# A trunk of two layers: weights split on ScalarE and VectorE in output projection and feed-forward, and norm products behind the up tiles

## The reference, cut to what matters

```python
for i in range(2):
    h = rms_norm(x, norm_g[i, 0])
    y = mixer(h)                          # ends with "@ w_out", 1024 x 1024
    x = x + rms_norm(y, norm_g[i, 1])     # "post" of sites 1 and 3
    y = conv_ffn(rms_norm(x, norm_g[i, 2]), ...)     # "pre" of sites 1 and 3
    x = x + rms_norm(y, norm_g[i, 3])     # "post" of sites 2 and 4

def conv_ffn(h, w_up, conv_w, conv_b, w_down):        # w_up 1024 x 5632, w_down 2816 x 1024
    u = causal_depthwise_conv(h @ w_up, conv_w, width=3) + conv_b
    val, gate = split(u, 2)
    return (gelu(gate) * val) @ w_down
```

## Time and profile before

| | us |
|---|---|
| median of 3 runs | 3966.37 |
| lowest and highest | 3961.04, 3982.27 |
| the profiled execution | 3962.33 |
| its span, first to last instruction | 3960.5 |
| TensorE busy | 3225.2 (81% of the span) |
| VectorE busy | 2469.7 (62%) |
| GpSimd busy | 1405.3 (35%) |
| ScalarE busy | 1367.3 (35%) |
| mean granted TensorE clock | 0.894 of full |

### The profile page before, as it was taken

How to read it: one execution, slowest core, us unless ns; L and a number is a source line. 1 busy time by engine, 2 the same in 40 slices (tenths; PEclk the granted TensorE clock), 3 DMA queues, 4 the chain that set the end, 5 groups by cost and what they waited for, 6 DMA issues and landing times. The chain is left out here.

```text
span 3960.5 us, 49368 instructions
## 1 busy us (share of the span) xinstructions
PE 3225.2 (81%) x16664; PEld 2657.6 (67%) x16664; DVE 2469.7 (62%) x3835; ACT 1367.3 (35%) x2987; POOL 1405.3 (35%) x1041
## 2 busy tenths in 40 slices
PE   7889989999879899879956401888888789998897
PEld 5778878888767777767744301766667668786786
DVE  5455555556278686678765698444442787867556
ACT  4255544445222222222234442444441322222222
POOL 2300000000356666657520000001015566775663
PEclk8699998899989999999987755989899899998998
DMA  4100000002322223223220000000023222232232
GB/s 150 43 1 16 16 18 16 16 16 96 107 68 87 75 85 96 81 73 91 80 77 11 11 0 0 16 32 16 32 96 122 69 80 85 85 96 75 84 101 77
DMA packets 281285, 237.45 MB, mean 60 GB/s; under 512 B 8533, under 2 KB 258071, under 8 KB 280599
## 3 DMA queue, kind: packets, MB, share of 16 engines
q1 hardware_dynamic: 279959, 233.17, 19.0%
q10 hardware_dynamic: 1152, 2.10, 0.1%
HBM read 205.88 MB, written 27.26 MB: 59 GB/s over the span
## 5 line engine op out<-in xcount | busy, mean ns | idle before, releaser
L377 PE MATMUL PS<-HH,WH 128*128 128x512 f32 x2160 | 896.1, 415 | 78.0 <-DVE HL L519 23.0
L366 POOL TENSOR_TENSOR WL<-WR,WH 128x1024 fp32r<-128x1024 f32 x335 | 873.1, 2606 | 27.9
L378 PE MATMUL PS<-HL,WH 128*128 128x512 f32 x2160 | 865.4, 401 | 0.0
L379 PE MATMUL PS<-HH,WL 128*128 128x512 f32 x2160 | 862.3, 399 | 0.0
L377 PEld LDWEIGHTS PS<-HH,WH 128*128 128x128 f32 x2160 | 422.3, 196 | 170.5 <-issue 57.2
L362 POOL TENSOR_TENSOR TOUCH<-WR 128x1 f32<-128x1 f32 x335 | 126.6, 378 | 1091.8 <-PE PS L379 893.2
L379 PEld LDWEIGHTS PS<-HH,WL 128*128 128x128 f32 x2160 | 420.3, 195 | 91.6
L378 PEld LDWEIGHTS PS<-HL,WH 128*128 128x128 f32 x2160 | 422.5, 196 | 85.2 <-issue 5.1
L363 POOL TENSOR_SCALAR WH<-WR 128x1024 fp32r<-128x1024 f32 x335 | 383.1, 1144 | 0.7 <-issue 0.3
L645 PE MATMUL PS<-m_KDH,m_QS 128*128 128x512 f32 (+2 forms) x192 | 93.0, 484 | 247.0 <-ACT m_PX L835 197.3
L978 POOL TENSOR_TENSOR n_ROT<-n_ROT,n_SIN 128x512 f32<-128x512 f32 x15 | 19.1, 1273 | 699.5 <-ACT n_ROT L617 699.5
(11 more groups left out here) (344 smaller groups left out, 6984.6 us busy)
## 6 DMA issues: line engine op xcount, KB each, us to landing
WR<-in_ffn_w_up SPq DMA_DIRECT2D x176, 512.0 KB, 3.8
WR<-in_ffn_w_down SPq DMA_DIRECT2D x88, 512.0 KB, 3.5
WR<-in_nsa_w_out SPq DMA_DIRECT2D x16, 512.0 KB, 3.8
WR<-in_dsa_w_in SPq DMA_DIRECT2D x16, 512.0 KB, 4.7
WR<-in_dsa_w_out SPq DMA_DIRECT2D x16, 512.0 KB, 3.9
WR<-in_nsa_w_in SPq DMA_DIRECT2D x15, 512.0 KB, 5.5
HH<-oh_save SPq DMA_DIRECT2D x2, 3584.0 KB, 12.5
HL<-ol_save SPq DMA_DIRECT2D x2, 3584.0 KB, 21.6
```

The source lines that it names most:

```text
L366: nc.gpsimd.tensor_tensor(WL[:, s, :], WR[:, r, :], WH[:, s, :].bitcast(F32), ALU.subtract).then_inc(w_split, 1)
L377: nc.tensor.matmul(dst, wh, xh, start=start, stop=False)
L378: nc.tensor.matmul(dst, wh, xl, start=False, stop=False)
L379: return nc.tensor.matmul(dst, wl, xh, start=False, stop=stop)
```

## The change

Output projection and feed-forward: GpSimd splits only the first three tiles of each output projection. For every other tile ScalarE copies the high part (`high_split_act`) and VectorE subtracts (`low_split_dve`), both written into their orders three tiles ahead: behind the eviction and the convolution of up tile t, and, for the second and third up tile of the next step, behind the down evictions. The tiny operation of line 362 falls away there. In attention and layer entry GpSimd goes on, its first tile waiting for the one before it.

Norm products of the feed-forward, and the output transposes, stand behind the up tiles of a step instead of ahead of them. The product of the second half's post norm moves from behind the first up tile to step 0, with its root and reciprocal. In the output projection the norm product of the pre norm stands behind k = 13 instead of 12, and VectorE's and ScalarE's norm work is cut up and chained to the tiles.

```diff
+        def high_split_act(act, info):
+            r, x = info["raw"], info["split"]
+            act.wait_ge(w_raw[r], info["landed"])
+            act.wait_ge(*info["free"])
+            act.wait_ge(w_hi, info["n"])
+            nc.scalar.activation(WH[:, x, :], WR[:, r, :], ACT.Copy).then_inc(w_hi, 1)
+
+        def low_split_dve(dve, info):
+            r, x = info["raw"], info["split"]
+            dve.wait_ge(w_hi, info["n"] + 1)
+            dve.wait_ge(w_split, info["n"])
+            nc.vector.tensor_tensor(WL[:, x, :], WR[:, r, :], WH[:, x, :].bitcast(F32),
+                                    ALU.subtract).then_inc(w_split, 1)
...
-                if k == DT + 4:
+                if k == DT + 5:
                     stat_pe(pe, 2 * n + 1, "pre", 0)
...
+            squares, highs = {2: (0, 3), 3: (3, 6), 4: (6, 8)}, {6: (0, 4), 7: (4, 8)}
...
                 nc.scalar.activation(Y[n][:, m, tokens(hf)], bank(k % 4), ACT.Copy).then_inc(out_ev, 1)
+                high_split_act(act, after_outproj(a, n, k))
...
+            applies, sums = {1: (0, 4), 2: (4, 8)}, {3: (1, 3), 4: (3, 8)}
+            products = {6: (0, 4), 7: (4, 8)}
+            for k in range(2 * DT):
+                hf, m = k // DT, k % DT
+                low_split_dve(dve, after_outproj(a, n, k))
+                if m:
+                    sum_dve(dve, site, "post", hf, m)
...
+                if m in applies:
+                    post_apply_dve(dve, site, 0, *applies[m])
+                for dt in range(*sums.get(m, (0, 0))):
+                    sum_dve(dve, site, "pre", 0, dt)
+                if m == 5:
+                    reciprocal_dve(dve, site, "pre", 0)
+                if m in products:
+                    d0, d1 = products[m]
+                    for dt in range(d0, d1 + 1):
+                        if dt < d1:
+                            pre_apply_dve(dve, site, 0, dt)
+                        if dt > d0:
+                            low_dve(dve, site, 0, dt - 1)
...
-                if g == 0 and t == 0:
-                    stat_pe(pe, 2 * n + 1, "post", 1)
...
         def ffn_pe(pe, n):
             up_pe(pe, n, 0)
             for g in range(GROUPS):
-                if g in STAT_POST and g:
+                if g + 1 < GROUPS:
+                    up_pe(pe, n, g + 1)
+                if g in STAT_POST:
                     stat_pe(pe, step_site(n, g), "post", STAT_POST[g])
...
-                if g + 1 < GROUPS:
-                    up_pe(pe, n, g + 1)
                 down_pe(pe, n, g)
...
+                    if ffn_place(g) + t + 3 < TILES:
+                        high_split_act(act, ffn_tile(n, ffn_place(g) + t + 3))
...
+            if ffn_place(g) + t + 3 < TILES:
+                low_split_dve(dve, ffn_tile(n, ffn_place(g) + t + 3))
...
                     up_act(act, n, g + 1)
+                    for b in range(ffn_place(g + 1) + 7, min(ffn_place(g + 1) + 9, TILES)):
+                        high_split_act(act, ffn_tile(n, b))
...
                     down_dve(dve, n, g, 5, 8)
+                    for b in range(ffn_place(g + 1) + 7, min(ffn_place(g + 1) + 9, TILES)):
+                        low_split_dve(dve, ffn_tile(n, b))
                     hidden_low_dve(dve, n, g + 1, 1)
...
-                    if g:
-                        reciprocal_dve(dve, site, "post", 0)
+                    reciprocal_dve(dve, site, "post", STAT_POST[g])
                     post_apply_dve(dve, site, STAT_POST[g], 0, 4)
```

More of the change, by code:

```diff
@@ L352, in load, with split @@
             sp.dma_start(dst, src).then_inc(w_raw[info["raw"]], 16)
-        def split(pool, info, it=0):
+        def split(pool, info, it=0, after=False):
             r, s = info["raw"], info["split"]
+            if after:
+                pool.wait_ge(w_split, info["n"])
             pool.wait_ge(w_raw[r], at(info["landed"], it))
@@ L1062, in outproj_pe, with after_outproj, outproj_act @@
                     stat_pe(pe, 2 * n + 1, "post", 0)
-                if k == DT + 4:
+                if k == DT + 5:
                     stat_pe(pe, 2 * n + 1, "pre", 0)
-        def outproj_act(act, n):
+        def after_outproj(a, n, k):
+            return a.infos["out"][k + 3] if k + 3 < 2 * DT else ffn_tile(n, k + 3 - 2 * DT)
+        def outproj_act(act, a, n):
             site = 2 * n + 1
+            squares, highs = {2: (0, 3), 3: (3, 6), 4: (6, 8)}, {6: (0, 4), 7: (4, 8)}
             for k in range(2 * DT):
@@ L1076, in outproj_act @@
                     root_act(act, site, "post", 0)
[L1077 to L1080, removed]
+                for dt in range(*squares.get(m, (0, 0))):
+                    pre_square_act(act, site, 0, dt)
+                if m == 5:
                     root_act(act, site, "pre", 0)
-                if m in (5, 6):
-                    for dt in range(4 * (m - 5), 4 * (m - 4)):
-                        high_act(act, site, 0, dt)
@@ L1086, in outproj_dve @@
-        def outproj_dve(dve, n):
+                for dt in range(*highs.get(m, (0, 0))):
+                    high_act(act, site, 0, dt)
+        def outproj_dve(dve, a, n):
             site = 2 * n + 1
-            for dt in range(1, DT):
-                sum_dve(dve, site, "post", 0, dt)
-            reciprocal_dve(dve, site, "post", 0)
[L1091 to L1107, removed]
+            applies, sums = {1: (0, 4), 2: (4, 8)}, {3: (1, 3), 4: (3, 8)}
[5 more added lines that the diff above has]
+                    sum_dve(dve, site, "post", hf, m)
+                if hf == 0:
+                    continue
+                if m == 0:
+                    reciprocal_dve(dve, site, "post", 0)
+                if m in applies:
+                    post_apply_dve(dve, site, 0, *applies[m])
+                for dt in range(*sums.get(m, (0, 0))):
+                    sum_dve(dve, site, "pre", 0, dt)
+                if m == 5:
+                    reciprocal_dve(dve, site, "pre", 0)
[6 more added lines that the diff above has]
+                            low_dve(dve, site, 0, dt - 1)
@@ L1137, in trunk, with ffn_tile, ffn_place @@
         APPLIES = {4: (1, 0, 3), 5: (1, 3, 6), 6: (1, 6, 8), 16: (0, 0, 3), 17: (0, 3, 6), 18: (0, 6, 8)}
+        def ffn_tile(n, b):
+            kind, g, c = ffn_order()[b]
+            return F[n][kind][g][c]
+        def ffn_place(g):
+            return 0 if g == 0 else 4 + 6 * (g - 1)
+        TILES = len(ffn_order())
         def step_site(n, step):
@@ L1386, in ffn_sp @@
                     load(sp, p["down"][g][c], wd[tile + c])
-        def ffn_pool(pool, n):
-            for kind, g, c in ffn_order():
-                split(pool, F[n][kind][g][c])
         def columns(w, col):
@@ L1730, in prep1_pool @@
         def prep1_pool(pool):
-            for x in L1["c"] + [L1["i0"]]:
+            split(pool, L1["c"][0], after=True)
+            for x in L1["c"][1:] + [L1["i0"]]:
                 split(pool, x)
@@ L2196, in _ @@
             attention_pool(pool, A0)
-            for x in L0["out"]:
+            for x in L0["out"][0:3]:
                 split(pool, x)
-            ffn_pool(pool, 0)
             prep1["pool"](pool)
             attention_pool(pool, A1)
-            for x in L1["out"]:
+            for x in L1["out"][0:3]:
                 split(pool, x)
-            ffn_pool(pool, 1)
         @block.scalar
@@ L2220, in _ @@
             attention_act(act, A0)
-            outproj_act(act, 0)
+            outproj_act(act, A0, 0)
             ffn_act(act, 0)
@@ L2224, in _ @@
             attention_act(act, A1)
-            outproj_act(act, 1)
+            outproj_act(act, A1, 1)
             ffn_act(act, 1)
```

7 lines of the change are left out of this document (2 added, 5 removed).

## The result

| | before | after |
|---|---|---|
| median | 3966.37 us (three runs; with the one taken beside the change 3963.7, 3948.67 to 3982.27) | 3804.78 us (four runs, 3791.11 to 3808.72) |
| ratio | | 0.9567, 95% interval 0.9528 to 0.9606 |
| profiled execution | 3962.33 | 3804.23 |
| its span | 3960.5 | 3802.4 |
| first up tile to last down, layers 0 and 1 | 825.9, 813.8 | 739.3, 741.6 |

The kernel became 4.3% faster. The forecast was 3820 us; the median lies inside the range of 3795 to 3875, the ratio applied to the 3966.4 of before gives 3794.6, just under its low end. The mechanism was right, the gain was under-sized: 143 us forecast, some 172 by the ratio (interval 156 to 187). The medians are nearer to each other, 3804.78 for 3963.7 (159 us), which lies at the low end of that interval.

What follows compares the result with a forecast made beforehand. TensorE was taken as the bound in a good step, with stalls and late downs as removable excess. Gains of 74 and 59 us in the feed-forwards and 10 in the projections made 143: 3820 us predicted, range 3795 to 3875.

Steps and rivals of the forecast that it cites:

- the sum of the new excess: Feed-forward time above 22 stall-free steps: 26 us left of 100.3 in layer 0, 29 of 88.2 in layer 1.
- The exclusion between GpSimd and VectorE: VectorE operations with two SBUF operands end only after GpSimd's 2.70 us subtraction, so its busy time is partly waiting.
- All stalls at norm products go: Feed-forward: all six TensorE stalls, 15 us each, covered by 21.8 us of up products; each product still costs 0.75.
- The charge for evictions: Third down eviction of a feed-forward step, slack 0.1 us: charged 0.3 us a step, 6 us a layer.
- Late downs in steps 1 and 13: Feed-forward: down starts 2 us late and loses 2.5 to the clock, 4.5 in each step, 9 a layer.
- The end of the feed-forward: Wait and low clock at the last down product, 7 us a layer before; 6 us a layer charged as remaining.
- Output projection: Stall moves rather than goes: 6.8 us at k = 13, normalized half complete at 61.6; gain 5 a layer, bounds -4 and 9.
- Third eviction late: Rival, 12%: the queue between second and third down eviction loses 1.4 us in each of 42 steps: 3866 us.
- Saturated by busy time: Rival, 3%: VectorE's 28 us a step are real work, 35 with the change, so it is the bound: 3852 us.
- Norm product waits elsewhere: Rival, 4%: sums still late behind the up tiles, so six stalls of 15 less the split's gain remain: 3905 us.
- Slower: Rival, 4%: VectorE becomes the bound if a subtraction of 1024 takes 2.7 us: 4018 us; decides from about 2.5 us.
- Better: Case, 10%: steps 1 and 13 lose nothing and the projection gains 9: 3794 us.

Runs made afterwards that it cites:

- the run with work nobody needs: Changed kernel plus two unused GpSimd subtractions of 640 columns per feed-forward weight tile: 4008.75 us, ratio 1.0102 to before.
- the one with the subtraction on GpSimd: Changed kernel with GpSimd instead of VectorE subtracting for the weights' low part, ScalarE still copying: 3893.73 us, ratio 0.9816 to before.
- the order alone: Kernel before, with only the feed-forward's up tiles moved ahead of norm products and transposes, GpSimd still splitting: 3914.57 us, ratio 0.9885.
- The longer subtraction: Changed kernel with half of each VectorE weight subtraction (512 columns) made once more ahead of it: 3878.19 us, ratio 0.976 to before.
- the split alone: Changed kernel with the feed-forward's norm products and output transposes ahead of the up tiles again: 3898.91 us, ratio 0.982 to before.
- the products one tile earlier: Changed kernel with all eight pre-norm products of the output projection directly behind the reciprocal, before tiles 14 and 15: 3773.41 us, ratio 0.9524 to before.
- the subtraction made twice: Changed kernel with each whole VectorE weight subtraction (1024 columns) made twice: 4024.73 us, ratio 1.0131 to before.

## Why the mechanism was right, and which terms were mis-sized

The step that failed is in the sum of the new excess, 26 us in layer 0 and 29 in layer 1, which came out at 13.7 and 16.0. Three of its terms were too large. The evictions were charged with 6 us a layer and cost 0.4; the late downs of steps 1 and 13 were charged with 9, 2.5 each of it for the clock, and cost 3.2 with no clock in it; the end was charged with 6 and waited 3.06 and some 2.5. What was to go, and why, was as forecast.

*The exclusion between GpSimd and VectorE: shown.* It was read from one pair of rows; the run with work nobody needs (204 us) shows it by itself, and the one with the subtraction on GpSimd (89 us) agrees, though a part of its price is that GpSimd's subtraction is longer. The Trainium skill (GPSIMD Engine Reference, Specifications) names the two parties; what the exclusion costs only the rows tell.

*The split hides: right.* Subtraction 1.21 assumed, 1.222 measured; copy 1.11 assumed, 1.063 measured. The down tiles' subtractions come in time in every good step, as walked.

*All stalls at norm products go: right,* and each product costs 0.86 us for the 0.75 assumed. But that they go does not by itself bring 15 us each: with the order alone a part came back as waits for evictions, and it gained 42 us, not 90. The sum's 15 a stall held only because the split was there too.

*The charge for evictions: wrong in size.* 6 us a layer, 12 in all, was charged as a safety on a slack of 0.1 us. Measured, TensorE's weight loads waited for those evictions 3.8 us in 19 places in layer 0, all at most 0.2, beside a busy PE: a down stretch is 11.38 us for 11.36, about 0.4 us a layer. The row of TensorE's weight-load waits in layer 0's feed-forward (us, times, longest):

```profile
PEld PS L395 <- DVE Y_b L1297: 3.8, 19, 0.2
```

The longer subtraction shows that the slack was real and small: 0.68 us more there, and the down stretch grew by 0.81.

*Late downs in steps 1 and 13: right place, wrong price.* 9 us a layer was charged, 2 late and 2.5 of clock each. Measured: 1.6 us late in each and no clock at all; the stretch behind took 11.45 us at full granted clock (2.4 GHz). 5.8 us a layer too much. Before, 2.17 us late had come with a low clock; the charge took the clock of that row over to these steps.

*The end of the feed-forward:* 6 charged; TensorE waited 3.06 us in layer 0 and 0.7 in layer 1 (there behind the 1.8 of the last transposes), and the clock stayed full behind the first of them. That the clock stayed full was luck of this execution: behind the same wait of 3.06 us the last down took 13.00 us at 0.87 with the split alone and 13.01 at 0.87 with the products one tile earlier, for 11.48 here. *Entry:* 2 charged, 2.8 measured. *Output transposes of layer 1:* 3.5 charged, 3.4 and one wait of 1.8 measured. Together with the charges above the remaining excess came to 13.7 and 16.0 us where the sum had 26 and 29: 25 of the 29 us between forecast and ratio. The largest mis-sized terms are the charge for evictions and that for steps 1 and 13, its clock above all.

*Output projection:* 5 forecast, 5.8 and 5.6 measured, with the two stalls about as walked (6.8 and about 12 forecast, 5.90 and 12.39 measured). What the prediction left unsaid is that 10 us a layer of it lay in the queue's order.

*The rivals.* Third eviction late: not so, 0.4 us. Saturated by busy time: refuted, with less work on VectorE its busy time stayed and the kernel slowed. Norm product waits elsewhere: not together with the split, but in part it is what the order alone does. Slower: not at 1.22 us; at 2.44 it happens, with the time that the rival gave for 2.7. Better: the outcome was nearest to this one (3794), though by another sum; steps 1 and 13 lost little, the evictions and the end gave the rest, and the projection did not.

*Open.* Why the longer subtraction hurts the steps with norm work, 2, 3, 14 and 15 among them, by 20 us a layer more than walked; how much of the 89 us is exclusion; and what makes the entry stretch differ by 29 us between the profiled executions, one of each kernel.

## What to carry to other kernels

Where two engines exclude each other, compare the minimum and median of one operation with both operands in SBUF with one that has an operand in PSUM before believing a busy time; moving work *onto* the busier engine can then shorten it. A wait taken out of a queue is worth its length only if the engine waited for has caught up by the next thing it must deliver: price the two together, by walking the queues. In an order written out by hand, a slack of 0.1 us held here in the steps whose every term was a measured row of the same shape, and the safety charge on it was wrong; for the steps with norm work the same kind of walk was some 20 us a layer short once the slack was used up.

## What the runs showed of the hardware

GpSimd and VectorE take turns instruction by instruction when both read two SBUF operands: 0.69 us became 1.74 beside GpSimd operations of 1.58, and up to 2.88 beside one of 2.70, with operands that have nothing to do with each other. The unneeded work cost 204 us for 835 us of GpSimd time (528 operations at a median of 1.58).

The clock's part in the price of a late down can be missing altogether, which the forecast had not allowed for. Two downs of the kernel with half a subtraction more, their first products and their windows (1.73 and 3.54 us late):

```profile
1287.91 0.47 PE L401 MATMUL PS<-HIDH_b,WH 128*128 128x512 f32 x1 [1.73 <-issue]
1250.66 0.48 PE L401 MATMUL PS<-HIDH_b,WH 128*128 128x512 f32 x1 [3.54 <-issue]
```

```profile
1287.91:1300.09 12.18, 11.69 (x49) 9.17 (x50) 8.86 (x13) 1.84 (x3) 0.00 (x0) 1.00 0.29 86
1250.66:1264.41 13.75, 13.26 (x49) 10.32 (x50) 8.87 (x13) 1.27 (x2) 0.00 (x0) 0.88 0.26 76
```

After the first the granted clock stays full and the stretch is as long as in a good step; after the second it is 0.88 and the stretch 1.57 us longer. But the length of one wait doesn't decide it alone. The last down of the changed kernel waited 3.06 us and ran at full clock too, while 2.17 us had come with a low one before. Its window:

```profile
1891.67:1903.15 11.48, 11.47 (x48) 8.94 (x48) 7.28 (x11) 3.69 (x6) 0.00 (x0) 1.00 0.35 92
```

Nor does the same wait in the same place always end alike: with the subtraction made twice, the down of step 7 came 2.47 us late in layer 0 and ran at 0.89 (14.10 us), and 2.46 late in layer 1 and ran at 1.00 (12.72). What else decides it these runs do not tell.
